# Gated DeltaNet inverse in 32x32 tiles for its first four rounds, and its first products moved into the last chunk of the in-projection

## What is computed

```python
kk = jnp.einsum('bhntd,bhnsd->bhnts', kc, kc)
m = jnp.where(strict, betac[..., :, None] * kk * gam, 0.0)
rhs = jnp.concatenate([vc * betac[..., None], kc * (betac * jnp.exp(bc))[..., None]], axis=-1)
sol = lax.linalg.triangular_solve(m + jnp.eye(CHUNK, dtype=F32), rhs, left_side=True,
                                  lower=True, unit_diagonal=True)
...
attn = jnp.einsum('bhntd,bhnsd->bhnts', qc, kc) * decay[None, :, None]      # retention
o_intra = jnp.einsum('bhnts,bhnsv->bhntv', attn, vc)
```

## Time and profile before

| | |
|---|---|
| median of 3 runs | 639.93 us (639.52 to 640.33) |
| the profiled execution | 640.08 us |
| its span | 638.3 us |
| PE busy | 549.9 us (86%) |
| DVE busy | 334.8 us (52%) |
| ACT busy | 245.9 us (39%) |
| POOL busy | 81.1 us (13%) |
| mean granted clock of PE | 0.942 |

### The profile page before, as it was taken

How to read it: one execution, slowest core, us unless ns; L and a number is a source line. 1 busy time by engine, 2 the same in 40 slices (tenths; PEclk the granted TensorE clock), 3 DMA queues, 4 the chain that set the end, 5 groups by cost and what they waited for, 6 DMA issues and landing times.

```text
span 638.3 us, 11981 instructions
## 1 busy us (share of the span) xinstructions
PE 549.9 (86%) x5109; PEld 456.6 (72%) x5109; DVE 334.8 (52%) x593; ACT 245.9 (39%) x455; POOL 81.1 (13%) x99
## 2 busy tenths in 40 slices
PE   2999987779889978695999999999999889978685
PEld 2999977679665644452999999899889665645452
DVE  2556759863633333237499655567455633333234
ACT  3555464435242313123544634433326243314121
POOL 6500243310100000001200380011010100000000
PEclk9999997779889989799899989999999799989799
DMA  8994400026978999998455342000105969999971
GB/s 313 279 336 141 164 2 1 1 100 248 394 277 349 408 408 409 409 398 291 132 198 197 87 150 67 3 3 4 67 1 225 409 260 356 408 409 409 409 312 67
DMA packets 55589, 145.24 MB, mean 228 GB/s; under 512 B 4212, under 2 KB 28992, under 8 KB 55408
## 3 DMA queue, kind: packets, MB, share of 16 engines
q1 hardware_dynamic: 54448, 142.47, 59.0%
q0 software_dynamic: 1088, 2.00, 1.4%
HBM read 143.40 MB, written 1.05 MB: 226 GB/s over the span
## 4 chain that ended last, share of the span: by engine, by line
PE 74%; DVE 12%; ACT 6%; issue 5%; DMA 2%; POOL 1%; SPq 0%; DVEq 0%; ACTq 0%
PE PS L1807 11%; PE PS L1769 7%; PE PS L495 7%; PE PS L497 6%; PE PS L496 6%; PE PS L1827 5%; PE PS L531 3%; PE PS L532 3%; PE PS L533 3%; PE PS L1840 3%; DVE WL L491 2%; PE PS L2099 2%; DVE X L1080 2%; DMA RAW<-ev_w_in 2%; PE PS L2120 1%
## 5 line engine op out<-in xcount | busy, mean ns | idle before, releaser
L491 DVE TENSOR_TENSOR WL<-RAW,WH 128x768 fp32r<-128x768 f32 (+2 forms) x96 | 82.9, 906 | 57.6 <-ACT WH L485 56.5
L495 PE MATMUL PS<-WH,HTH 128*128 128x384 f32 (+2 forms) x272 | 91.2, 335 | 3.1 <-DVE HTL L1080 1.4
L497 PE MATMUL PS<-WH,HTL 128*128 128x384 f32 (+2 forms) x272 | 89.8, 330 | 0.0
L496 PE MATMUL PS<-WL,HTH 128*128 128x384 f32 (+2 forms) x272 | 89.8, 330 | 0.0
L485 ACT ACTIVATE WH<-RAW 128x768 fp32r<-128x768 f32 (+2 forms) x96 | 70.8, 796 | 18.4 <-PE PS L497 10.3
L1080 DVE TENSOR_TENSOR YL<-PS,YH 128x512 fp32r<-128x512 f32 x36 | 24.9, 691 | 73.4 <-ACT YH L860 71.5
L1080 DVE TENSOR_TENSOR X<-PS,X 128x512 f32<-128x512 f32 (+2 forms) x84 | 52.3, 660 | 18.1 <-PE PS L497 12.9
L1807 PE MATMUL PS<-RAW,GT 128*32 128x256 f32 (+1 forms) x544 | 42.8, 435 | 19.4 <-issue 18.8
L495 PEld LDWEIGHTS PS<-WH,HTH 128*128 128x128 f32 x272 | 52.5, 193 | 4.7 <-DVE HTL L1080 2.2
L1807 PEld LDWEIGHTS PS<-RAW,GT 128*32 128x32 f32 (+1 forms) x544 | 25.5, 130 | 39.4 <-issue 30.6
L496 PEld LDWEIGHTS PS<-WL,HTH 128*128 128x128 f32 x272 | 52.7, 194 | 0.0
(11 more groups left out here) (339 smaller groups left out, 1057.3 us busy)
## 6 DMA issues: line engine op xcount, KB each, us to landing
RAW<-moe_w_gate SPq DMA_DIRECT2D x34, 512.0 KB, 8.3
RAW<-moe_w_up SPq DMA_DIRECT2D x34, 512.0 KB, 9.1
RAW<-moe_w_down SPq DMA_DIRECT2D x34, 512.0 KB, 9.2
XG<-moe_w_gate SPq DMA_DIRECT2D x32, 512.0 KB, 12.4
XG<-moe_w_up SPq DMA_DIRECT2D x32, 512.0 KB, 13.4
XD<-moe_w_down SPq DMA_DIRECT2D x32, 512.0 KB, 14.7
RAW<-od_w_in SPq DMA_DIRECT2D x9, 1536.0 KB, 7.5
RAW<-ev_w_in SPq DMA_DIRECT2D x6, 1536.0 KB, 12.9
```

The lines of the kernel that those rows point to most:

```text
L491: done(nc.vector.tensor_tensor(out=lo, in0=raw, in1=hi.bitcast(F32), op=ALU.subtract), "unit_lo")
L495: nc.tensor.matmul(ps, ah, bh, start=start, stop=False)
L496: nc.tensor.matmul(ps, ah, bl, start=False, stop=False)
L497: return nc.tensor.matmul(ps, al, bh, start=False, stop=stop)
```

## The change

On PE the retention scores of heads 0 and 1 now follow the second unit of chunk 9, and the key scores of heads 4 to 7 the third; the second retention scores come after T of round 1. On ACT the copies of chunk 8 come after the exponent. On DVE both calls of `negated` come first, and the products of the retention scores after them. T now writes banks 4 and 5, and Z banks 0 and 1. In rounds 1 to 4 each block of 64 is taken as two products of 32x32 on its diagonal, four for each head and half (`quarters`), in T, Q and Z. ACT's copies and DVE's placements keep their shapes.

```diff
--- before.py
+++ after.py
@@ -496,7 +496,7 @@
             nc.tensor.matmul(ps, ah, bl, start=False, stop=False)
             return nc.tensor.matmul(ps, al, bh, start=False, stop=stop)
 
-        def project(pe, layer, what, c):
+        def project(pe, layer, what, c, inside=lambda c, j: None):
 
             kind, _, w = (CHUNKS[layer] if what == "in" else OUT_CHUNKS)[c]
             n_out = NT if kind == "tok" else w // P
@@ -506,6 +506,7 @@
                 if c == 0:
                     pe.wait_ge(sem("hT_lo"), 8 * layer + (4 if what == "out" else 0) + j + 1)
                 project_unit(pe, layer, what, c, j)
+                inside(c, j)
 
         def project_unit(pe, layer, what, c, j):
 
@@ -787,10 +788,12 @@
                         inside(c, j)
                     if c == 0:
                         lhs_hi(2 * layer)
-                    else:
+                    elif not layer or c < n - 1:
                         evacuate(layer, c - 1)
                     split_hi(act, i, 3)
                     between(c)
+                if layer:
+                    evacuate(layer, n - 2)
                 evacuate(layer, n - 1)
 
             def out_split(layer, n):
@@ -1013,7 +1016,7 @@
             def inverse_X(g, L):
                 rows = slice(0, P if L < 6 else CH)
                 act.wait_ge(sem(f"c_T{g}"), L)
-                done(nc.scalar.activation(heads(XC, g)[rows], level_ps(0, g)[rows], ACT.Copy), f"c_X{g}")
+                done(nc.scalar.activation(heads(XC, g)[rows], level_ps(4, g)[rows], ACT.Copy), f"c_X{g}")
 
             def inverse_Q(g, L):
                 rows = slice(0 if L < 6 else CH, P)
@@ -1531,8 +1534,8 @@
             def negated(g):
                 dve.wait_ge(sem("c_kk"), g + 1)
                 if g:
+                    done(stt(NTD[:, 4:6, :], PS[:, 4:6, 0:384], -1.0, GA[:, 4:6, :], MUL, MUL), "c_nt")
                     done(stt(NTD[:, 6:8, :], PS[:, 2:4, 0:384], -1.0, GA[:, 6:8, :], MUL, MUL), "c_nt")
-                    done(stt(NTD[:, 4:6, :], PS[:, 4:6, 0:384], -1.0, GA[:, 4:6, :], MUL, MUL), "c_nt")
                 else:
                     done(stt(NTD[:, 0:4, :], PS[:, 4:8, 0:384], -1.0, GA[:, 0:4, :], MUL, MUL), "c_nt")
                 dve.wait_ge(sem("c_nt"), 2 * g + 1)
@@ -1546,7 +1549,7 @@
             def inverse_level(g, L):
 
                 dve.wait_ge(sem(f"c_Z{g}"), L)
-                z = PS[:, 4 + g, :].rearrange("p (i h t) -> p i h t", i=2, h=4)
+                z = PS[:, g, :].rearrange("p (i h t) -> p i h t", i=2, h=4)
                 hs = slice(4 * g, 4 * g + 4)
                 if L < 6:
                     done(nc.vector.copy_predicated(YC[:, :, hs, :],
@@ -1598,11 +1601,11 @@
             dve.wait_ge(sem("c_yi"), 2)
             dve.wait_ge(sem("maskc"), 2)
             negated(0)
-            dve.wait_ge(sem("proj_ev"), proj_total[1])
+            negated(1)
             chunk_done(dve, 1, "in", len(CHUNKS[1]) - 1)
             retention_scores(0)
-            negated(1)
             retention_scores(1)
+            dve.wait_ge(sem("proj_ev"), proj_total[1])
             inverse_level(0, 1)
             inverse_level(1, 1)
             dve.wait_ge(sem("d_O"), 2)
@@ -1701,10 +1704,10 @@
                     pe.wait_ge(sem("par_in"), 16 * N_PAR)
                     done(nc.tensor.transpose(PS[:, 7, 0:78], ROWS[0:78, :], ident[0:78, 0:78]), "pt_ps")
 
-            def in_projection(layer, between):
+            def in_projection(layer, between, inside=lambda c, j: None):
                 lhs(lambda i, k: H[:, i, k * P:(k + 1) * P], lambda i: pe.wait_ge(sem("h"), 2 * layer + i + 1))
                 for c in range(len(CHUNKS[layer])):
-                    project(pe, layer, "in", c)
+                    project(pe, layer, "in", c, inside)
                     between(c)
 
             def out_units(layer, units):
@@ -2038,7 +2041,13 @@
                     pe.wait_ge(sem("c_silu"), 4)
                     key_scores(0)
 
-            in_projection(1, layer1_small)
+            def layer1_inside(c, j):
+                if (c, j) == (9, 1):
+                    pe.wait_ge(sem("c_nt"), 1)
+                    retention_scores(0)
+                if (c, j) == (9, 2):
+                    pe.wait_ge(sem("proj_ev"), outs_before[1, "in", 9])
+                    key_scores(1)
 
             def retention_scores(r):
                 if r:
@@ -2049,6 +2058,8 @@
                     mm(PS[:, 6 + h % 2, 0:T], k[:, 0:P], q, start=True, stop=True)
                     last = mm(PS[:, 6 + h % 2, T:384], k[:, P:T], q[:, P:T], start=True, stop=True)
                 done(last, "d_S")
+
+            in_projection(1, layer1_small, layer1_inside)
 
             def retention_out():
                 pe.wait_ge(sem("d_at"), 4)
@@ -2080,6 +2091,7 @@
                 done(last, "c_qkp")
 
             low, high = halves = [slice(0, CH), slice(CH, P)]
+            quarters = [(slice(32 * a, 32 * a + 32), 32 * (a % 2)) for a in range(4)]
 
             def where(b, i, h):
 
@@ -2090,20 +2102,30 @@
 
             def inverse_T(g, L):
                 if L == 1:
+                    pe.wait_ge(sem("c_nt"), 2)
                     pe.wait_ge(sem("c_ones"), 2 * g + 2)
                 else:
                     pe.wait_ge(sem(f"c_Y{g}"), L - 1)
                 for i, h in group(g):
-                    b, cs = where(0, i, h)
-                    for rows in halves if L < 6 else (low,):
-                        last = mm(PS[rows, b, cs], YC[rows, i, h, :], ident[rows, rows], start=True, stop=True)
+                    b, cs = where(4, i, h)
+                    if L < 5:
+                        for rows, o in quarters:
+                            last = mm(PS[rows, b, cs][:, o:o + 32], YC[rows, i, h, o:o + 32], ident[rows, rows], start=True, stop=True)
+                    else:
+                        for rows in halves if L < 6 else (low,):
+                            last = mm(PS[rows, b, cs], YC[rows, i, h, :], ident[rows, rows], start=True, stop=True)
                 done(last, f"c_T{g}")
 
             def inverse_Q(g, L):
                 pe.wait_ge(sem(f"c_X{g}"), L)
                 for i, h in group(g):
                     b, cs = where(2, i, h)
-                    if L < 6:
+                    if L < 5:
+                        for rows, o in quarters:
+                            n = 256 * i + rows.start
+                            last = mm(PS[rows, b, cs][:, o:o + 32], NTD[rows, h, n:n + 32], XC[rows, i, h, o:o + 32],
+                                      start=True, stop=True)
+                    elif L < 6:
                         for c, rows in enumerate(halves):
                             last = mm(PS[rows, b, cs], NTD[rows, h, 256 * i + CH * c:256 * i + CH * c + CH], XC[rows, i, h, :],
                                       start=True, stop=True)
@@ -2114,8 +2136,12 @@
             def inverse_Z(g, L):
                 pe.wait_ge(sem(f"c_Qs{g}"), L)
                 for i, h in group(g):
-                    b, cs = where(4, i, h)
-                    if L < 6:
+                    b, cs = where(0, i, h)
+                    if L < 5:
+                        for rows, o in quarters:
+                            last = mm(PS[rows, b, cs][:, o:o + 32], QC[rows, i, h, o:o + 32], YC[rows, i, h, o:o + 32],
+                                      start=True, stop=True)
+                    elif L < 6:
                         for rows in halves:
                             last = mm(PS[rows, b, cs], QC[rows, i, h, :], YC[rows, i, h, :], start=True, stop=True)
                     else:
@@ -2158,18 +2184,15 @@
             def mixed(i, k):
                 return TM[:, i, k * P:(k + 1) * P] if k < 4 else TM[:, i, 1552 + (k - 4) * P:1552 + (k - 3) * P]
 
-            pe.wait_ge(sem("c_nt"), 1)
-            retention_scores(0)
-            pe.wait_ge(sem("proj_ev"), proj_total[1])
-            key_scores(1)
-            retention_scores(1)
-            pe.wait_ge(sem("c_nt"), 3)
             for L in range(1, 7):
                 inverse_T(0, L)
                 inverse_T(1, L)
+                if L == 1:
+                    retention_scores(1)
                 inverse_Q(0, L)
                 inverse_Q(1, L)
                 if L == 1:
+                    pe.wait_ge(sem("proj_ev"), proj_total[1])
                     retention_out()
                 inverse_Z(0, L)
                 inverse_Z(1, L)
```

## The result

The changed kernel takes 658.15 us (median of 4 runs, 657.76 to 659.14); the kernel before took 640.13 on the same chip (4 runs, 639.52 to 641.21). The ratio is 1.028 (1.026 to 1.030): 18 us slower, where 6 us faster was forecast.

A forecast was written before the change was run, and what follows sets the result against it. PE was taken to bound the kernel (74% of the chain), with copy latency next once PE is faster. Rounds 2 to 4 -4.5 and front with round 1 -1.5, -6.1 with rounding, from 639.93 give 633.8 us, range 632.0 to 639.5.

The forecast's parts named there:

- What one record costs in a 32x32 tile: PE products of the inverse: four diagonal tiles overlap, 8.2 ns a record, so a group's 64 records take 0.52 us.
- rival 2: Tile products on PE: only two row tiles run at a time, 16 ns a record, 641.3 us; chance 0.07.
- Rounds 2 to 4: T, Q and Z of the inverse: rounds of 5.36, 5.04 and 5.04 us, together 15.44 against 19.98, -4.5 us.
- one group's way: A step's latency in the rounds: 0.52 issue, 0.27 until ACT starts, 0.60 copy, 0.07 back, 1.46 us.
- Front and round 1: Last in-projection chunk to T of round 2: earlier exponent and reordered scores bring T to 415.27 from 416.80, -1.5 us.
- Rival 1: T, Q, Z of four rounds: fixed time per record whatever its tile, 29.2 ns, 660.5 us; chance 0.13.
- The argument "against": Against a fixed record time on PE: 58.8 ns halves exactly with two tiles, and four tiles ran at once in the experts.
- The two pages of the Trainium skill: PE matmuls: some 60 cycles each however few columns, floor about 25 ns start to start; 654 us by that sum.
- Rival 3: New rounds: part is lost, records of 10 to 14 ns or a low-clock stretch as PE pauses, 635.4 to 637.0; chance 0.18.

The follow-up runs named there:

- one-pass kernel: Kernel before plus only the 32x32 tiles, their products (T of round 1 excepted) reading a bf16 identity, one weight load and one record each: 639.73 us, ratio 0.998.
- kernel of the wider products: Kernel before plus only the 32x32 tiles, each of their products with 64 moving columns in place of 32: 659.72 us against 641.76, ratio 1.032.

## Why the prediction was wrong

- *What one record costs in a 32x32 tile*: right. 8.2 ns was forecast, 8.9 measured in a block that is there, at the full clock. So rival 2, with 16 ns, falls.
- *Rounds 2 to 4*, "a step is no longer 2 x 0.52 = 1.04 but one group's way": this step failed. The sum counted PE's time and the latency of the copies, and no cost of bringing instructions. The missing term is 784 instructions at 3.72 / 256 = 14.5 ns, 11.4 us a round, and it takes the place of the others: 13.18, 11.56 and 10.76 us measured for 5.36, 5.04 and 5.04. Whether the sum was good for what it counted isn't shown. The one-pass kernel comes near it, 5.58, 5.82 and 4.89 (16.3 for 15.4), but with half of the records and a granted clock of 0.50 to 0.61, two differences that work against each other; that the totals meet is luck.
- *Front and round 1*, -1.5: in the changed kernel T of group 1 came at 409.11 and the retention output at 412.23. The whole profile is 1.2 us late before the change begins (key scores of group 0 at 397.12 for 395.95), so they lie within 0.3 of the forecast (407.7 and 410.8). Then the first stop made the retention output 3.88 us long (412.23 to 416.11) for the forecast's 2.87, and of the 1.5 only 0.2 was left at T of round 2. With 64x64 products the front is worth 0.0.
- *Rival 1*, the issue as the floor: 660.5 us, for 658.15. Its total is near by luck, since its mechanism was wrong. A record has no fixed time of its own. 29.2 ns for the densest group before is the array's (half of one tile's 58.8, with no stop in those rounds), and the supply's 3.72 us for 128 records is 29.1, by chance the same. So the rival has rounds 2 to 4 nearly right, +16.8 for +15.5, but puts +3.8 on round 1, which lost nothing, and nothing on round 5, which lost 1.2. A hint was in the profile of before: 41 instruction packets of 16 KB, in the rounds as little as 3.7 us apart. The argument "against" (58.8 halves exactly) spoke only of the array.
- The two pages of the Trainium skill cited against the change gave 654. Their sign was right; the 8.9 ns show that their floor for a product, about 25 ns or 60 cycles, isn't paid here. Another page was not drawn on: the Trainium skill, "Runtime: NRT & Kernel Launch" (Instruction fetch mechanics), states that the sequencer fetches blocks of 16 KiB by itself and that the cost of crossing into one is "mostly hidden". The kernel before agrees, with 5.8 us of supply in a round of 6.6; the changed kernel doesn't, with 11.4.
- *Rival 3*, the low clock: it came, first at 421.84 us, behind the stop of 2.18, and costs the 1.2 us of round 5. That pauses as such bring it isn't borne out: the kernel of the wider products stops at the same numbers, with PE busy 7.58 of 12.00 us at a granted clock of 1.00, and the one-pass kernel has hardly a stop and 0.50 to 0.61. What lowered it stays open.

## What to carry to other kernels

Count TensorE's instructions in a stretch, not only its columns: an fp32 product is four of them whatever its size, and here no stretch went faster than 256 in 3.5 to 4 us. Cutting each product into two smaller tiles doubles that count for the same work; look at the page's instruction queue, and in the timeline for "issue" ahead of the middle of a group, which no semaphore explains. A stretch close to the limit can't be made faster by a cheaper product; what helped here took a whole step off the engine (rounds of 5.2 to 6.0 us for 6.6).

## What had not been expected of the hardware

- Instruction blocks of 256 arrive one in 3.46 to 4.0 us when TensorE is waiting for them, at either level of the clock and at a DMA share of 0.03. The packet itself takes 0.9 to 1.5 us of that; the rest is 1.0 to 1.1 us from the end of a stop to the next packet's start, and 1.3 to 1.6 us from a packet's end to the end of the stop (the eight stops of the changed kernel). Why these two are so long no run shows.
- A semaphore increment by TensorE costs 116 ns (1496 of them, eleven in a row, added 173.8 us).
- Products of 64 rows and one column between 64x64 ones: 0.47 us each, at a granted clock of 0.50.
- VectorE transposes 32x32 blocks of 128x512 fp32 in 0.71 us, about as long as the placement of `YC` of that shape (0.73).
